# Feed-forward gate and up: h_hi and h_lo as one moving operand of 512 columns for w_hi

## The reference

```python
def swiglu_2(x, w_gate, w_up, w_down):
    return (jax.nn.silu(x @ w_gate) * (x @ w_up)) @ w_down
```

## Time and profile before

| | us |
|---|---|
| median of 3 runs | 1777.5 (1775.33 to 1777.9) |
| the profiled execution | 1775.59 |
| its span, first to last instruction | 1773.8 |
| mean granted TensorE clock | 0.955 of 2.4 GHz |

### The profile page before, as it was taken

How to read it: one execution, slowest core, us unless ns; L and a number is a source line. 1 busy time by engine, 2 the same in 40 slices (tenths; PEclk the granted TensorE clock), 3 DMA queues, 4 the chain that set the end, 5 groups by cost and what they waited for, 6 DMA issues and landing times.

```text
span 1773.8 us, 29357 instructions
## 1 busy us (share of the span) xinstructions
PE 1659.2 (94%) x12004; PEld 1512.9 (85%) x12004; DVE 1002.7 (57%) x1307; ACT 842.7 (48%) x1280; POOL 63.3 (4%) x73
## 2 busy tenths in 40 slices
PE   7879778989999899998689999999999999999999
PEld 6768658879999899987579999899989977789998
DVE  4844665556545645565755455654568834565554
ACT  6534144554444544455344444544457653554443
POOL 0200000000000000000200000000000004200000
PEclk9889979999999999999799999999999995799999
DMA  6320024435555455544215555455534540055553
GB/s 243 126 89 2 6 91 155 143 107 190 189 189 183 149 182 187 178 179 152 95 72 190 185 186 178 171 183 186 190 143 167 192 164 24 32 183 181 187 180 115
DMA packets 37080, 263.68 MB, mean 149 GB/s; under 512 B 4224, under 2 KB 4352, under 8 KB 5760
## 3 DMA queue, kind: packets, MB, share of 16 engines
q1 hardware_dynamic: 35712, 257.97, 40.5%
q0 software_dynamic: 704, 2.62, 0.4%
q10 hardware_dynamic: 576, 1.84, 0.3%
HBM read 261.36 MB, written 1.05 MB: 148 GB/s over the span
## 4 chain that ended last, share of the span: by engine, by line
PE 88%; DVE 7%; ACT 3%; issue 1%; DMA 1%; SPq 0%; POOLq 0%; POOL 0%; DVEq 0%; ACTq 0%
PE PS L398 26%; PE PS L399 25%; PE PS L400 25%; PE PS L618 2%; PE PS L641 2%; PE PS L938 1%; DVE w_lo L1424 1%; PE PS L392 1%; DMA raw_weights<-W 1%; PE PS L503 1%; PE PS L527 1%; DVE arena L1671 1%; PE PS L917 1%; PE PS L916 1%; PE PS L611 0%
## 5 line engine op out<-in xcount | busy, mean ns | idle before, releaser
L1424 DVE TENSOR_TENSOR w_lo<-raw_weights,w_hi 128x1024 fp32r<-128x1024 f32 x488 | 598.9, 1235 | 549.3 <-ACT w_hi L987 549.0
L987 ACT ACTIVATE w_hi<-raw_weights 128x1024 fp32r<-128x1024 f32 x488 | 512.8, 1059 | 537.2 <-PE PS L400 520.4
L398 PE MATMUL PS<-h_hi,w_hi 128*128 128x256 f32 x2320 | 663.2, 286 | 17.4 <-DVE h_lo L1450 10.3
L399 PE MATMUL PS<-h_lo,w_hi 128*128 128x256 f32 x2320 | 659.7, 284 | 0.0
L400 PE MATMUL PS<-h_hi,w_lo 128*128 128x256 f32 x2320 | 659.5, 284 | 0.0
L398 PEld LDWEIGHTS PS<-h_hi,w_hi 128*128 128x128 f32 x2320 | 448.5, 193 | 23.5 <-issue 7.9
L399 PEld LDWEIGHTS PS<-h_lo,w_hi 128*128 128x128 f32 x2320 | 448.6, 193 | 2.0 <-issue 0.2
L400 PEld LDWEIGHTS PS<-h_hi,w_lo 128*128 128x128 f32 x2320 | 448.4, 193 | 0.0
L398 PE MATMUL PS<-w_hi,g_hi 128*128 128x512 f32 x440 | 171.8, 390 | 0.0
L399 PE MATMUL PS<-w_lo,g_hi 128*128 128x512 f32 x440 | 171.8, 390 | 0.0
L400 PE MATMUL PS<-w_hi,g_lo 128*128 128x512 f32 x440 | 171.2, 389 | 0.0
(11 more groups left out here) (340 smaller groups left out, 1305.8 us busy)
## 6 DMA issues: line engine op xcount, KB each, us to landing
raw_weights<-W SPq DMA_DIRECT2D x244, 1024.0 KB, 4.8
post_gain<-post_gains POOLq DMA_DIRECT2D x3, 512.0 KB, 3.9
x_resid<-x SPq DMA_DIRECT2D x2, 512.0 KB, 6.7
arena<-mem POOLq DMA_DIRECT2D x1, 1024.0 KB, 5.5
out<-x_resid SPq DMA_DIRECT2D x2, 512.0 KB, 2.6
ptab<-cols ACTq DMA_DIRECT2D x1, 857.0 KB, 8.8
ctab<-consts ACTq DMA_DIRECT2D x1, 758.0 KB, 5.7
rtab<-rows ACTq DMA_DIRECT2D x1, 176.0 KB, 11.4
```

The source lines that it names most:

```text
L398: mm(out, lhs[0], rhs[0], start=start, stop=False)
L399: mm(out, lhs[0], rhs[1], start=False, stop=False)
L987: A(w_hi[:, n % H, :], raw[:, n % (2 * R), :], ACT.Copy).then_inc(S.hi_ready, 1)
L1424: v.tensor_tensor(w_lo[:, n % H, :], raw[:, n % (2 * R), :], w_hi[:, n % H, :].bitcast(F32), ALU.subtract).then_inc(S.lo_ready, 1)
```

## The change

`h_hi` and `h_lo` become the two halves of one tensor, `h_both`. A new `wide_slot` takes the place of `feat_slot` for gate and up in the feed-forwards only. Each half of 128 features now has a PSUM bank of its own: per chunk one matmul of 512 columns (`w_hi` against the chunk of `h_hi` and that of `h_lo`) fills the bank's two halves, and one of 256 columns (`w_lo` against `h_hi`) adds to the first half; in the last chunk these two are in the other order. A gate takes two banks and an up two. Block 0 uses banks 0 to 3, all others banks 4 and 5 for the gate and 6 and 7 for the up. VectorE adds the two halves of each bank with a `tensor_reduce` over a stride of 256 words: the gate sum into `sg` after it has split up to n+4, the up sum into `up`, which lies in `xn`. Silu now reads and writes `sg`, and the product takes `up` from SBUF. The waits are new: from b = 2 on TensorE waits for the gate sum of the block before ahead of a gate and for `g_mult` of the block before ahead of an up; ScalarE waits for `gate_sum` ahead of silu; VectorE waits for its own up sum.

```diff
-        h_hi = sb("h_hi", KC * T, F32R)[:].rearrange("p (c t) -> p c t", c=KC)
-        h_lo = sb("h_lo", KC * T, F32R)[:].rearrange("p (c t) -> p c t", c=KC)
+        h_both = sb("h_both", 2 * KC * T, F32R)[:].rearrange("p (s c t) -> p s c t", s=2, c=KC)
+        h_hi, h_lo = h_both[:, 0, :, :], h_both[:, 1, :, :]
...
+        up = xn[:, 0, 0:512]
...
         def gate_bank(b):
-            return 4 + 2 * (b % 2) if b else 0
+            return 4 if b else 0
+
+        def two_sums(bank):
+            return PS[:, bank:bank + 2, :].rearrange("p j (s t) -> p j t s", s=2)
...
+            def wide_slot(n, bank, i=0, normed=None):
+                for j in range(2):
+                    pe.wait_ge(S.lo_ready, LOOP * i + n + j + 1)
+                    both_out = PS[:, bank + j, :].rearrange("p (s t) -> p s t", s=2)
+                    for c in range(KC):
+                        if normed is not None and j == 0:
+                            pe.wait_ge(S.hT_ready, 8 * normed + c + 1)
+                        cs = slice(c * P, (c + 1) * P)
+                        hi, lo = w_hi[:, (n + j) % H, cs], w_lo[:, (n + j) % H, cs]
+                        if c < KC - 1:
+                            mm(both_out, hi, h_both[:, :, c, :], start=c == 0, stop=False)
+                            mm(PS[:, bank + j, 0:T], lo, h_hi[:, c, :], start=False, stop=False)
+                        else:
+                            mm(PS[:, bank + j, 0:T], lo, h_hi[:, c, :], start=False, stop=False)
+                            mm(both_out, hi, h_both[:, :, c, :], start=False, stop=True).then_inc(S.half_done, 1)
...
                     if b >= 2:
-                        pe.wait_ge(S.act_ready, ii * 2 + (NB * f + b - 1))
-                    feat_slot(ffn_half(f, "G", b), gate_bank(b), i, None if b else k)
-                    feat_slot(ffn_half(f, "U", b), gate_bank(b) + 1, i)
+                        pe.wait_ge(S.gate_sum, ii * 2 + (NB * f + b))
+                    wide_slot(ffn_half(f, "G", b), gate_bank(b), i, None if b else k)
+                    if b >= 2:
+                        pe.wait_ge(S.g_mult, ii * 2 + (NB * f + b))
+                    wide_slot(ffn_half(f, "U", b), gate_bank(b) + 2, i)
...
                     split(n + 4, i)
-                    act.wait_ge(S.half_done, LOOP * i + n + 2)
-                    if b >= 2:
-                        act.wait_ge(S.act_ready, ii * 2 + (NB * f + b - 1))
-                    A(sg[:, b % 2, :], PS[:, gate_bank(b), :], ACT.Silu).then_inc(S.silu_ready, 1)
+                    act.wait_ge(S.gate_sum, ii * 2 + (NB * f + b + 1))
+                    A(sg[:, b % 2, :], sg[:, b % 2, :], ACT.Silu).then_inc(S.silu_ready, 1)
...
                     n = ffn_half(f, "G", b)
+                    jt = lambda ap: ap.rearrange("p (j t) -> p j t", j=2)
+                    split(n + 4, i)
+                    dve.wait_ge(S.half_done, LOOP * i + n + 2)
+                    v.tensor_reduce(jt(sg[:, b % 2, :]), two_sums(gate_bank(b)), AX.X, ALU.add).then_inc(S.gate_sum, 1)
                     split(n + 6, i)
                     dve.wait_ge(S.half_done, LOOP * i + n + 4)
+                    v.tensor_reduce(jt(up), two_sums(gate_bank(b) + 2), AX.X, ALU.add).then_inc(S.up_sum, 1)
+                    dve.wait_ge(S.up_sum, ii * 2 + (NB * f + b + 1))
                     dve.wait_ge(S.silu_ready, ii * 2 + (NB * f + b + 1))
-                    v.tensor_tensor(sg[:, b % 2, :], sg[:, b % 2, :], PS[:, gate_bank(b) + 1, :], ALU.mult)\
-                        .then_inc(S.g_mult, 1)
+                    v.tensor_tensor(sg[:, b % 2, :], sg[:, b % 2, :], up, ALU.mult).then_inc(S.g_mult, 1)
```

More of the change, by code:

```diff
@@ L231, in build_program @@
                  "params_loaded x_loaded mem_loaded pos_loaded out_stored dve_step ssq_ready ms_ready "
-                 "std_ready xn_ready xT_ready hT_ready silu_ready act_ready yssq_ready yms_ready ystd_ready "
+                 "std_ready xn_ready xT_ready hT_ready silu_ready gate_sum up_sum act_ready yssq_ready yms_ready ystd_ready "
                  "zero_ready ka_ready bonus_ready   pad_ready pin_ready glu_ready q_mixed lora_ready wa_done g_done decay_ready a_ready g_ready "
```

## The result

The changed kernel takes 1762.16 us (median of 4 runs, 1760.58 to 1762.84), the kernel before beside it 1776.41 (1774.3 to 1777.9). The ratio is 0.9918, 95% interval 0.9902 to 0.9934: faster by 14.3 us or 0.8%. The forecast was 1755 with a range of 1751 to 1760. The direction was right, the size was not: 22.2 us were forecast and 14.3 came, and the time lies above the range.

What follows compares the result with a forecast made beforehand. TensorE's matmul pace was taken as the bound: 1760 chunks x 0.0129 us = 22.7 us, less 0.5 for late places, net 22.2, so 1777.5 - 22.2 = 1755.3, rounded to 1755 us. Range 1751 to 1760.

Steps and rivals of the forecast that it cites:

- What bounds the kernel: In the feed-forward loop only the number and pace of TensorE's matmuls set the time; a block takes 16.98 us.
- After: 0.2269 + 0.1199 = 0.3468 us: Per chunk of gate and up, one wide plus one narrow matmul, 0.0129 us less than three narrow ones at 0.3597.
- Two-piece moving operand: Wide matmul's read of h_both in two runs of 256 words: cost taken as 0, worst end +0.09 us.
- Sums and banks: Two VectorE sums per block at 1.22 us each, 2.44 at worst; banks not doubled and new waits cost 0.
- margin of the last block: Last block of each feed-forward: g_lo done 1.0 us before its down starts; at worst 0.2 us late, five times.
- The rule of about 2.5 ns: Skill's fixed cost per warm matmul; by it 1760 fewer matmuls would save 4.4 us.
- A: Two-run read in wide matmuls breaks overlap of weight load and matmul: 158 us less 22, about 1914 us; chance 0.05.
- B: Surcharge on gate and up matmuls is paid per run, not per matmul: nothing gained, 1777.5 to 1778; chance 0.04.
- C: Most surcharge stays with columns or banks; a warm matmul saves 2.5 of 13 ns: 1773 us; chance 0.02.
- D: VectorE becomes the bound in the block if a sum takes 4.0 us; slower from 4.2 us; chance 0.01.
- E: Matmul sum holds, but last blocks, sums and shifted stretches of falling clock cost more: 1757 to 1762; chance 0.08.
- The sign that was named for A and B: In gate and up, a wide matmul's start-to-start of 0.24 us or more would point to A or B.

Runs made afterwards that it cites:

- the control run: The changed kernel with the wide matmul split again into two of 256 columns, new banks, sums and waits kept: 1777.4 us, ratio 1.0006 to the kernel before.
- the equal widths: The changed kernel, adjacent layout, from each half's second chunk on two matmuls of 384 columns, part of the computation left out: 1754.37 us, ratio 0.9878.
- the strict kernel: The changed kernel without the other order in the last chunk, so wide and narrow matmuls alternate through every half: 1765.38 us, ratio 0.9935.
- runs of two: The changed kernel with two wide then two narrow matmuls, four times per half, first gate half alternating: 1754.87 us, ratio 0.9877.
- the grouping: The changed kernel with each half's eight wide matmuls first, then its eight narrow ones: 1762.5 us, ratio 0.9929.

## Why the prediction was wrong, point by point

- **What bounds the kernel**: right. TensorE's matmuls in gate, up and down, before and after; the change of the block is the whole gain between the profiled executions.
- **The step that failed** is the term "After: 0.2269 + 0.1199 = 0.3468 us". Both paces were read in runs of equal width and then added for a sequence that alternates. The mechanism (one surcharge of 13.3 ns less per chunk) was right, and it showed at 256, 384 and 512 columns; its size in this sequence was not: 0.3522 in place of 0.3468, 7.5 ns saved per chunk in place of 12.9. That is 9.5 us. The kernel before had the evidence: the wide pace of 0.2279 just behind up, which the prediction took for a second value of the same thing ("its first ones start 0.23 apart") and for an end of the range. It was a transient of 27 ns behind a change of width, and the change puts seven such changes from narrow to wide into each half. It warned of the cost but did not give its size: with only the first steps behind each change (233 + 113) a pair comes to 346, with the whole transient (27 less 7) to 367, and 352.2 was measured.
- **Two-piece moving operand**: right, cost 0.
- **Sums and banks**: right. 1.225 us each (1.22 forecast), VectorE 10.92 us a block (11.1), margin of the last block 1.6 us (1.0), no wait of TensorE on the sums; the control run has the block of the kernel before.
- **The rule of about 2.5 ns** per warm matmul (the Trainium skill, TensorE: Matmul & The Clock Gate, "Wait — 56ns, not 53.3ns?"): the trace disagrees with it here, at three widths; it would have given 1773. That the measured gain lies between its 4.4 us and the 22.2 is chance: what was saved is 13.3 ns less the excess of the alternation.
- **The rivals**: A, B, C and D fell; the saving was smaller, but not for C's reason, as the equal widths show. E gave 1757 to 1762, and 1762.16 at its edge is chance: the last blocks and the sums cost nothing, and its stretches at a lower clock did shift, for the 1.6 us above, but came out even in sum. The sign that was named for A and B, a wide step of 0.24 or more, was nearly met (0.235 in the mean, single steps of 0.241) and would have pointed at the wrong cause. None of the rivals had a cost of alternating, although the change's whole point is an alternating sequence. The range (1751 to 1760) left out the time because both of its ends were made from runs of one width.

**What stays open** is what the phase is made of. The runs show that the sequence of widths and the way in which TensorE enters it set the pace, and that layout, order of writes and the number of matmuls don't; the same transient in down, in other banks, speaks against the banks. Which entry leads to which pace is known only for the cases above. Each matmul in these runs has a weight load of its own, and none varied that. In the strict kernel a load's recorded start lies 2 to 5 ns behind that of the matmul ahead of it at either pace, so the loads do not tell the two apart. Which part of the engine holds that phase isn't shown.

## What to carry to other kernels

A pace of matmuls read from a run of one width holds for that width in a row; before it is added into a mixed sequence, look in the trace for a place where the width changes. A transient there says that the sum can be off, by up to the whole transient at each change; how much of it a short run pays had to be measured here. Where wide and narrow matmuls must mix, try the order of the widths: runs of two took back 4 of the 5.6 ns that alternating costs a pair, for a reordering of two lines. A median that doesn't move can hide effects of both signs: only the block and the first half, read apart, showed that the grouping gained 0.11 us a block and lost 0.54 us at the start of the first feed-forward.

## What the runs showed of the hardware that was not expected

- Alternating 512 and 256 columns at the full clock ran at 346.7 ns a pair or at 353.3 (a pattern of three pairs: 233, 117, 241, 120, 236, 113), with the same instructions. Behind an idle gap of TensorE it ran at 346.7 in 44 of 45 gates that followed 512-column matmuls, and at 353.3 in all five that followed an alternating up.
- Behind a narrow run the wide matmuls take 233, 236, 229, 232, 231 ns before they settle at 226.7; behind a wide run the first narrow one takes 113 in place of 120.
- A tensor_reduce over pairs 256 words apart in PSUM (128x1024) takes 1225 ns; a tensor_tensor that reads as much of PSUM in one piece took 1221 in the kernel before.
- A TensorE wait for its own last matmul lengthened the step from start to start from 0.227 to 0.53 or 0.63 us, and the next one by 0.1.
